# A two-layer mLSTM/GLA, sparse attention and expert kernel: transposes, rope, low parts and residual quarters of the second layer in another order

## The reference, cut to what matters

```python
def dsa_mixer(x, positions, w_in, w_out):
    q, k, v, qi, ki, wi = split_cols(x @ w_in, ODD_SPLITS)
    q = partial_rotary(q..., positions, ROPE_DIM)        # 16 heads of 128
    k = partial_rotary(k..., positions, ROPE_DIM)        # 4 heads of 128
    qi = partial_rotary(qi..., positions, IDX_ROPE_DIM)  # 16 index heads of 64
    ki = partial_rotary(ki..., positions, IDX_ROPE_DIM)  # 1 index key head
    ...                                     # then for each query:
    idx_logits = einsum('bqhd,bsd->bqhs', qib, ki)
    score = einsum('bqhs,bqh->bqs', relu(idx_logits), wib)   # masked, causal
    _, sel = lax.top_k(score, 64)
    ...                                     # softmax attention over sel only
    return out.astype(x.dtype) @ w_out

for layer in range(DEPTH):
    mix = ab_mixer(h, ...) if layer % 2 == 0 else dsa_mixer(h, positions, ...)
    h = layer_norm(DEEPNORM_ALPHA * h + mix, ...)
    h = layer_norm(DEEPNORM_ALPHA * h + moe_ffn(h, ...), ...)
```

## Time and profile before

| | us |
|---|---|
| median of three runs (lowest, highest) | 1774.95 (1772.21, 1775.88) |
| profiled execution, whole | 1774.51 |
| its span, first to last instruction | 1772.7 |
| TensorE busy with matmuls | 1605.2 (91%) |
| VectorE busy | 720.2 (41%) |
| ScalarE busy | 466.2 (26%) |
| mean granted TensorE clock | 0.971 |

### The profile page before, as it was taken

The page is one execution under the profiler, slowest core; times in us unless marked ns, Lnnn a source line. Parts: engine busy times, 40 slices in busy tenths (PEclk is TensorE's granted clock), DMA queues, the critical chain, the costliest instruction groups (busy, mean ns, idle before and its releaser), DMA issues.

```text
span 1772.7 us, 18355 instructions
## 1 busy us (share of the span) xinstructions
PE 1605.2 (91%) x7223; PEld 953.4 (54%) x7223; DVE 720.2 (41%) x1212; ACT 466.2 (26%) x692; POOL 16.8 (1%) x36
## 2 busy tenths in 40 slices
PE   8999999998999889899879899999899988989975
PEld 6888887875433325333238778877543332533321
DVE  6675564656211121111167697655621112111116
ACT  4565535432200001000034335553220000100000
POOL 1000000000000000000000000000000000000000
PEclk9999999998999999999989899999899999989998
DMA  9666554783899999999985455549389999999995
GB/s 269 170 187 180 166 154 143 261 308 151 355 416 421 421 416 421 410 421 421 419 298 159 122 166 165 156 125 338 145 352 418 421 422 416 421 407 422 421 419 238
DMA packets 133269, 538.12 MB, mean 304 GB/s; under 512 B 19376, under 2 KB 19504, under 8 KB 86848
## 3 DMA queue, kind: packets, MB, share of 16 engines
q1 hardware_dynamic: 132608, 532.75, 79.1%
q0 software_dynamic: 576, 4.19, 0.6%
HBM read 534.82 MB, written 2.10 MB: 303 GB/s over the span
## 4 chain that ended last, share of the span: by engine, by line
PE 56%; issue 29%; DMA 10%; DVE 3%; ACT 1%; SPq 1%; POOL 0%; POOLq 0%; DVEq 0%; ACTq 0%
PE ps L750 12%; PE ps L752 11%; PE ps L751 11%; PE ps L1035 8%; DMA ring<-in_moe_w_down 5%; PE ps L1097 4%; DMA ring<-in_moe_w_up 4%; PE ps L731 1%; PE ps L1015 1%; PE ps L1016 1%; PE ps L1024 1%; PE ps L1207 1%; PE ps L1221 1%; PE ps L1179 0%; DMA arena<-in_x 0%
## 5 line engine op out<-in xcount | busy, mean ns | idle before, releaser
L750 PE MATMUL ps<-w_lo,x_hi 128*128 128x512 f32 x880 | 351.3, 399 | 12.8 <-DVE w_lo L1764 5.4
L1764 DVE TENSOR_TENSOR w_lo<-ring,w_hi 128x1024 fp32r<-128x1024 f32 x224 | 270.2, 1223 | 193.9 <-ACT w_hi L1314 192.4
L751 PE MATMUL ps<-w_hi,x_hi 128*128 128x512 f32 x880 | 345.4, 393 | 0.0
L1314 ACT ACTIVATE w_hi<-ring 128x1024 fp32r<-128x1024 f32 x224 | 235.5, 1058 | 314.9 <-PE ps L752 314.8
L2206 DVE TENSOR_TENSOR arena<-ps,arena 128x512 f32<-128x512 f32 x128 | 83.0, 687 | 417.7 <-PE ps L1025 417.7
L750 PEld LDWEIGHTS ps<-w_lo,x_hi 128*128 128x128 f32 x880 | 166.7, 189 | 53.2 <-issue 7.9
L751 PEld LDWEIGHTS ps<-w_hi,x_hi 128*128 128x128 f32 x880 | 166.8, 189 | 34.8 <-issue 0.5
L1035 PE MATMUL ps<-arena,hT 128*64 128x512 f32 x768 | 175.6, 612 | 8.1 <-DVE hT L2196 4.3
L1097 PE MATMUL ps<-ring,arena 128*64 128x512 f32 x768 | 170.2, 594 | 5.0 <-DMA ring<-in_moe_w_down 5.0
L1522 ACT ACTIVATE y_hi<-ps 128x512 fp32r<-128x512 f32 x64 | 36.1, 596 | 458.4 <-PE ps L1097 240.9
L752 PE MATMUL ps<-w_hi,h_lo 128*128 128x512 f32 x384 | 149.8, 390 | 0.0
(11 more groups left out here) (332 smaller groups left out, 1538.3 us busy)
## 6 DMA issues: line engine op xcount, KB each, us to landing
arena<-in_moe_w_gate SPq DMA_DIRECT2D x48, 2048.0 KB, 18.4
ring<-in_moe_w_down SPq DMA_DIRECT2D x96, 1024.0 KB, 18.3
arena<-in_moe_w_up SPq DMA_DIRECT2D x32, 2048.0 KB, 20.4
ring<-in_moe_w_up SPq DMA_DIRECT2D x32, 2048.0 KB, 20.9
ring<-in_ab_w_in SPq DMA_DIRECT2D x96, 512.0 KB, 3.7
ring<-in_moe_w_gate SPq DMA_DIRECT2D x16, 2048.0 KB, 20.4
arena<-in_moe_w_down SPq DMA_DIRECT2D x32, 1024.0 KB, 18.1
ring<-in_c_w_in SPq DMA_DIRECT2D x64, 512.0 KB, 3.6
```

What stands on the lines that cost most here:

```text
L750: nc.tensor.matmul(t, x_h, w_l[:, k, :], start=(opens and k == 0), stop=False)
L751: nc.tensor.matmul(t, x_h, w_h[:, k, :], start=False, stop=False)
L1314: act.activation(high_unit(n), raw_unit(n)[0], ACT.Copy).then_inc(w_hi_ready, 1)
L1764: v.tensor_tensor(lo, raw, high_unit(n).bitcast(FP32), ALU.subtract).then_inc(w_lo_ready, 1)
```

## The change

Six edits, all of order and none of arithmetic:

1. The index transposes `qiT` move in front of the last unit (23) of chunk 2, on TensorE and in the tile plan; ScalarE's copies of them move before its high part 27 and VectorE's behind low part 24. In the plan the tiles of chunk 2 now come after `qiT`, which gives them banks 6 and 7 in place of 1 and 2; the elder tiles there are chunk 1's (ScalarE drains them), where they were the hidden state's transposes.
2. The keys' rope on VectorE moves behind the 12 index evictions, the `kT` transposes on TensorE behind unit 26, ScalarE's `kT` copy behind high part 30, VectorE's behind the first long sum.
3. Between the long sums stand two low parts each time in place of one, and one behind the last; so the top-k rounds take low parts 34 to 41 along.
4. The scale and shift of the hidden state goes by quarters (eight pairs of 512-column ops) with low parts 12 to 19 between, and low parts 16 to 19 are gone from their old place. No engine waits for `h_ready`, which the second op of each pair raises.
5. At the end of the mixer `add_residual(1, 0)` stands behind low part 80 in place of 83.
6. At the program's start ScalarE does the sines behind the first two input tiles and high parts 0 and 1.

```diff
     plan += [("xT1", 8, "D" * 8), ("chunk1_0", 2, "AA"), ("small1", 1, "D")]
-    plan += [("chunk1_1", 2, "AA"), ("small1T", 1, "D"), ("chunk1_2", 2, "AA")]
-    plan += [("qiT", 5, "ADADA"), ("index", 12, "D" * 12), ("kT", 2, "AD")]
+    plan += [("chunk1_1", 2, "AA"), ("small1T", 1, "D"), ("qiT", 5, "ADADA"), ("chunk1_2", 2, "AA")]
+    plan += [("index", 12, "D" * 12), ("kT", 2, "AD")]
     plan += [("chunk1_3", 2, "AA"), ("chunk1_4", 2, "AA")]
...
             last.then_inc(psum_full, 1)
-            chunk(1, 2)
+            units(1, 16, 23)
             pe.wait_ge(roped, 1)
             for i in range(5):
                 transposes("qiT", i, [QIN[:, tt, 2 * n:2 * n + 2, :].rearrange("p a b -> p (a b)") for n in (2 * i, 2 * i + 1) if n <= IH // 2
                                       for tt in range(TT)])
+            units(1, 23, 24)
             wait_tiles("qiT", 5)
...
                 index_pair(i, 0, 2 * (i - 8))
+            units(1, 24, 27)
             pe.wait_ge(roped, 2)
             for i in range(2):
                 transposes("kT", i, [QN[:, tt, 2 * GQ + 2 * i + j, :] for j in range(2) for tt in range(TT)])
-            for c in (3, 4):
-                chunk(1, c)
+            units(1, 27, 40)
 
...
 
-            act.wait_ge(trig_in, 1)
-            act.activation(sinv[:, :, :].rearrange("p a b -> p (a b)"), kf[:, 0, :], ACT.Sin)
-            act.activation(cosv[:, :, :].rearrange("p a b -> p (a b)"), kf[:, 1, :], ACT.Sin).then_inc(trig_out, 1)
             for quad in range(4):
                 tokens_hi("xT0", (2 * quad, 2 * quad + 1), x_hi_ready)
                 high_parts(0, 2 * quad, 2 * quad + 1)
+                if quad == 0:
+                    act.wait_ge(trig_in, 1)
+                    act.activation(sinv[:, :, :].rearrange("p a b -> p (a b)"), kf[:, 0, :], ACT.Sin)
+                    act.activation(cosv[:, :, :].rearrange("p a b -> p (a b)"), kf[:, 1, :], ACT.Sin).then_inc(trig_out, 1)
             act.wait_ge(gate_w_loaded, 48)
...
             projected(1)
-            high_parts(1, *range(20, 28))
-            projected(2)
+            high_parts(1, *range(20, 27))
             for i in range(0, 5, 2):
                 act.wait_ge(psum_full, filled("qiT", i))
                 n = 2 if i < 4 else 1
                 act.activation(qiT[:, 2 * i:2 * i + n, :].rearrange("p a b -> p (a b)"), tile("qiT", i)[:, 0:n * SEQ], ACT.Copy)\
                    .then_inc(drained["A"], 1)
+            high_parts(1, 27)
+            projected(2)
+            high_parts(1, *range(28, 31))
             act.wait_ge(psum_full, filled("kT", 0))
             act.activation(qT[:, 2 * GQ:2 * GQ + 2, :].rearrange("p a b -> p (a b)"), tile("kT", 0)[:, :], ACT.Copy).then_inc(drained["A"], 1)
-            high_parts(1, *range(28, 36))
+            high_parts(1, *range(31, 36))
             projected(3)
...
             v.wait_ge(xhat_by_act, 4)
-            for n in range(2 * TT):
-                tt, cols = n // 2, slice(n % 2 * 2 * BANK, (n % 2 + 1) * 2 * BANK)
+            for n in range(4 * TT):
+                tt, cols = n // 4, slice(n % 4 * BANK, (n % 4 + 1) * BANK)
                 link(v.tensor_tensor(h[:, tt, cols], acc[:, tt, cols], ln_gb2[:, 0, cols], ALU.mult))
...
 
-            low_parts(1, *range(16, 20))
             wait_projected(1)
             v.wait_ge(drained["D"], drained_by[:first["small1T"] + 1].count("D"))
             rope(QIN, rope_t, 0, IDH // 8, 16)
-            low_parts(1, *range(20, 28))
-            wait_projected(2)
-            rope(QN[:, :, 2 * GQ:2 * GQ + KVH, :], rope_t, 1, DH // 8, 0)
+            low_parts(1, *range(20, 25))
             for i in (1, 3):
                 v.wait_ge(psum_full, filled("qiT", i))
                 v.tensor_copy(qiT[:, 2 * i:2 * i + 2, :].rearrange("p a b -> p (a b)"), tile("qiT", i)[:, :]).then_inc(drained["D"], 1)
-
-            v.wait_ge(roped, 2)
+            low_parts(1, 25, 26)
+
             for tt, lo, hi in ((1, 0, 8), (0, 8, 12)):
...
                      .then_inc(drained["D"], 1)
+            wait_projected(2)
+            rope(QN[:, :, 2 * GQ:2 * GQ + KVH, :], rope_t, 1, DH // 8, 0)
+            low_parts(1, 27, 28)
+            v.wait_ge(drained["D"], drained_by[:first["index"] + 12].count("D"))
+            v.reduce_sum(score[:, 1, 0:P], R[:, :, 0:P].rearrange("p a b -> p b a"), AX.X)
             v.wait_ge(psum_full, filled("kT", 1))
             v.tensor_copy(qT[:, 2 * GQ + 2:2 * GQ + 4, :].rearrange("p a b -> p (a b)"), tile("kT", 1)[:, :]).then_inc(drained["D"], 1)
-            low_parts(1, 28, 29)
-            v.wait_ge(drained["D"], drained_by[:first["index"] + 12].count("D"))
-            v.reduce_sum(score[:, 1, 0:P], R[:, :, 0:P].rearrange("p a b -> p b a"), AX.X)
-            low_parts(1, 30)
+            low_parts(1, 29, 30)
             link(v.reduce_sum(score[:, 1, P:SEQ], R[:, :, P:SEQ].rearrange("p a b -> p b a"), AX.X))
-            low_parts(1, 31)
+            low_parts(1, 31, 32)
             link(v.reduce_sum(score[:, 0, 0:P], R0[:, :, :].rearrange("p a b -> p b a"), AX.X))
+            low_parts(1, 33)
             for tt in range(TT):
...
                 link(ins)
-                low_parts(1, 32 + n)
+                low_parts(1, 34 + n)
             for tt in range(TT):
...
             rope_heads(0)
-            low_parts(1, *range(40, 46))
+            low_parts(1, *range(42, 46))
             turned_q(0)
...
             scale_router(1)
-            low_parts(1, *range(79, 84))
+            low_parts(1, 79, 80)
             add_residual(1, 0)
-            low_parts(1, 84)
+            low_parts(1, *range(81, 85))
             add_residual(1, 1)
...
```

## The result

The changed kernel takes 1760.3 us (median of 4 runs, 1758.77 to 1762.0) where the kernel before took 1774.12 beside it (4 runs): ratio 0.9922, 95% interval 0.9907 to 0.9937. A second set of runs of the same kernel gave 1759.09 us and 0.9914 [0.9901, 0.9926]. The forecast was 1759.4. The profiled execution has a span of 1757.9 us for 1772.7. One execution of a kernel further down (index_alone) took 3493.94 us, twice the time of the others, for a reason that no run shows; it is left out of the ratios.

What follows compares the result with a forecast made beforehand. TensorE was taken to bound layer 1's mixer, each hole costing its length plus lower clock behind it. Gains 2.3 + 4.7 + 3.4 + 4.95 = 15.3 off 1774.5 gave 1759.2, stated as 1759.4 us; range 1755.5 to 1765.5.

Steps and rivals of the forecast that it cites:

- A: Unit 16 in layer 1's mixer: TensorE's 2.00 us idle for its low part shrinks; gain 2.3 us, at worst 0.5.
- The new wait on the bank: Unit 16: chunk 2's first tile waits for ScalarE's copy of chunk 1, leaving about 1.5 of the 2.00 us idle.
- the clock's part: Unit 16: the lower TensorE clock followed the 2.00 us idle but would not follow one of 1.5.
- B: Index stage: the 3.44 us wait for qiT copies goes and index matmuls run at full clock; gain 4.7 us.
- C: Unit 32: the wait for low part 32, behind three long sums and the first top-k round, goes; gain 3.4 us.
- D: Unit 80: the wait for the residual sum goes; gain 4.95 us, 3.1 of it wait and 1.85 lower clock.
- The start: Program start: high parts 0 and 1 come earlier and a second table load is covered; gain 0.
- rival 1: Lower clock follows one or both 1.5 us holes, 1.7 us each: 1761 to 1763 us; chance 0.22.
- rival 2: VectorE doesn't keep up around low parts 33 and 34, costing up to 3.4 us: 1761 to 1763; chance 0.12.
- Rival 3: Bank waits on ScalarE at unit 16 and index tile 6 keep the holes, 3 us less gain: 1762; chance 0.08.
- experts' stream: Behind the mixer, the experts' DMA stream takes gain back: 1768 us, or the same time if all is lost; chance 0.05.
- the clock never stayed low over units 16 to 23: Rival that the lower clock stays through units 16 to 23, 21.8 us more: 1781 us; chance 0.02.

Runs made afterwards that it cites:

- index_alone: Kernel before with only the index transposes ahead of unit 23, their bank plan, and the later keys' rope and kT: 1771.59 us, ratio 0.9984.
- no_quarters: Changed kernel with the hidden state's scale and shift by halves again and low parts 16 to 19 in their old place: 1761.16 us, ratio 0.9915.
- start_alone: Kernel before with only the sines moved behind the first input tiles at the program's start: 1773.24 us, ratio 0.9996.
- no_sums: Changed kernel with one low part again between the long sums and the top-k rounds from low part 32 on: 1761.95 us, ratio 0.9928.
- no_tail: Changed kernel with the first residual sum back behind low part 83: 1766.09 us, ratio 0.9947.
- twice: Changed kernel with ScalarE's two copies of chunk 1 done twice, only the second pair releasing the banks: 1763.93 us, ratio 0.9935.

## Why the prediction was right, point by point

- **A, 2.3 forecast.** From `small1`, high part 20 comes at 26.5 in place of 28.5: 2.07. The new wait on the bank was forecast at 1.5 and is 1.58, and quarters take 0.68 to 0.69 (0.66 taken). no_quarters gives 2.13. The step that doesn't stand is the clock's part. Length was said to decide, with 2.00 enough; index_alone and start_alone show 2.00 at the full clock. Against those two the changed kernel's high part 20 comes only 0.47 earlier (26.49 for 26.95 and 26.96), which is what the shorter idle is worth. The other 1.6 of A are there in two of four profiles, and that the profile of before was one of them is luck.
- **B, 4.7 forecast.** Unit 24 starts 54.21 us behind `small1`; it was 61.08 with the later `kT` taken off. That is 6.87 for A and B, 7.0 forecast, and B is 4.8; index_alone against start_alone gives 4.77, with the same clock at unit 16 in both. The first eviction comes 1.16 behind the first matmul (1.3 taken), and the hole before unit 24 is 1.28 (1.5). The copies of chunk 2 were in time.
- **C, 3.4 forecast.** High part 36 is 10.28 earlier against `small1`, 3.41 over A and B; no_sums gives 3.49. The slack at low part 34 was put at 0.9: it ends at 1038.7 (the row at 1037.49 above) and the first matmul of unit 34 is at 1040.18 in the timeline, 1.5.
- **D, 4.95 forecast.** 7.67 - 2.72 = 4.95; no_tail gives 5.10. ScalarE waits 3.0 for the load of unit 85 (1.6 forecast), TensorE not at all. The load took 13.8 us where it took 12.5. The forecast put its length down to the expert step of 2 MB ahead of it; GpSimd issues two loads of 1 MB just then as well (at 1196.63 and 1197.21 before), and no run tells their shares apart.
- **The start, 0 forecast.** Right in sum, wrong in course: it was said that unit 0 could not start earlier, but it starts at 11.95 in place of 12.38. The clock eats it: eight matmuls run at the lower level before it rises, where it was four.

```profile
10.72 1.28 ACT L1346 ACT_TABLE_LOAD   x1
12.01 0.24 ACT L1346 ACTIVATE sinv<-arena 128x48 f32<-128x48 f32 x1
```

The second table load took 1.28 and the sine followed 0.01 behind it, so the price from the earlier trace rows held; the copy behind it came at 12.29, 0.43 later (0.7 forecast). The drain of 1.38 that the Trainium skill, "ScalarE: Activation LUTs", section "What ACT_TABLE_LOAD costs", adds is not seen here either.

- **The rivals.** The lower clock behind the two short holes (rival 1) stands in none of the five profiles that have the 1.58 or the ten that have the 1.28. VectorE too late (rival 2) came only once the bank waits were out too. Rival 3 named the bank waits, which are there but as small as worked out. Nothing was taken back by the experts' stream (no_tail), and the clock never stayed low over units 16 to 23.

So the single undoings (2.13, 3.49, 5.10) and B's 4.8 add up to 15.5, the 15.53 measured in the stretch; the medians show 13.8 and 15.7. Without the lower clock at unit 16 of the profile before it would be 13.9, so 1.6 of the agreement in this sum is luck. The last step of the forecast has a slip: 1759.2 and the 0.4 by which that execution lies under the median make 1759.6, not 1759.4.

## What to carry to other kernels

Price each hole by following the work released behind it, and read what is late next: here each of the four gains came out within 0.3 us, in profiles where the clock fell as it had before. The new bank waits deserved attention too: of 2.9 us of them, another list of bank numbers took 1.7 out of the stretch. Add a lower clock to a hole's price only as a chance, and compare kernels over a stretch between two fixed events, since outside it the profiles here differ by up to 3.7 us; look at the whole time as well, since what is given back outside the stretch stands only there. When two engines each have little slack, removing the last wait of one only shows the other.

## What the runs showed of the hardware that was not expected

- Whether the lower clock comes with an idle is a draw: before and start_alone have the same mixer, and the idle of 2.00 has it in the one and not in the other. Idles of 2.00 at unit 16: two of four profiles with the lower clock. 2.8 to 3.1 at unit 32: one of four. 3.1 at unit 80: four of four. 3.44 before the index matmuls: two of two. 2.84 in twice: its one profile. Idles of 1.58 (five) and 1.28 (ten): none. With counts as small as these it stays open whether the odds differ by place.
- At layer 1's start the same instructions took 36.3 to 39.0 us, by how long the clock stayed low. The window 926 to 930 us in start_alone and in the changed kernel:

```profile
926.00:930.00 4.00, 4.00 (x20) 3.27 (x19) 3.97 (x8) 1.07 (x1) 0.00 (x0) 1.00 0.30 78
```

```profile
926.00:930.00 4.00, 4.00 (x11) 3.13 (x10) 3.96 (x7) 0.00 (x0) 0.00 (x0) 0.50 0.00 0
```

In the first 20 matmuls run, at 1.00 of the clock, in the second 11 at 0.50.
